# Three sets of transposes taken from TensorE to VectorE and a DRAM scratch, and 384 partial sums dealt anew, in a two-block transformer kernel

## The reference, cut to what matters

```python
q = (_rmsnorm(c_q, q_norm) @ w_qb).reshape(b, s, MLA_HEADS, MLA_QK)      # first block, layer 1
q_rope = _rope(q_rope, cos[:, :, None, :], sin[:, :, None, :])           # 16 heads x 64
mod = c_act @ w_ada[l] + b_ada[l]                                        # 2048 -> 6 x 2048, one row
qa = apply_rope(rms_norm(qa, q_norm_w[l]), cos, sin)                     # second block, 8 heads x 128
merged = jax.nn.sigmoid(ga) * (ya @ w_oa[l]) + jax.nn.sigmoid(gb) * (yb @ w_ob[l])
x = x + g1 * (merged @ w_out[l])
```

## Time and profile before

| | |
|---|---|
| median of three runs | 2192.4 us |
| the profiled execution, own time | 2195.33 us |
| its span | 2193.4 us |
| TensorE busy | 2170.4 us, 99% |
| VectorE busy | 1514.1 us, 69% |
| ScalarE busy | 1019.5 us, 46% |
| moved by DMA | 512.22 MB, mean 234 GB/s |
| granted clock of TensorE | 0.998 of 2.4 GHz |

### The profile page before, as it was taken

One profiled execution on the slowest core, in us unless ns is written; L12 is line 12 of the kernel. 1 busy time (PEld: TensorE's weight loads), 2 busy tenths in 40 slices (PEclk: granted clock), 3 DMA queues, 4 the chain that ended last, 5 costly groups with the idle time before them and its releaser, 6 DMA issues.

```text
span 2193.4 us, 32090 instructions
## 1 busy us (share of the span) xinstructions
PE 2170.4 (99%) x10814; PEld 1840.6 (84%) x10814; DVE 1514.1 (69%) x2046; ACT 1019.5 (46%) x1251; POOL 297.4 (14%) x555
## 2 busy tenths in 40 slices
PE   9999999999999999999999999999999999999998
PEld 8898888988778887899888888888888888888886
DVE  6766668877777877688776768776666666554544
ACT  5445544554444546434555544454444444444433
POOL 2101110112220010701110211111111111000000
PEclk9999999999999999999999999999999999999999
DMA  8877577688996584968766887767878887765564
GB/s 291 240 193 245 174 260 245 198 227 287 299 297 190 176 303 143 263 204 263 229 187 193 285 277 239 237 222 237 268 253 278 268 260 241 224 233 185 190 198 139
DMA packets 204124, 512.22 MB, mean 234 GB/s; under 512 B 32704, under 2 KB 60000, under 8 KB 203744
## 3 DMA queue, kind: packets, MB, share of 16 engines
q1 hardware_dynamic: 166256, 394.10, 56.3%
q0 software_dynamic: 37456, 115.92, 16.6%
q10 hardware_dynamic: 288, 0.52, 0.1%
HBM read 502.58 MB, written 7.91 MB: 233 GB/s over the span
## 4 chain that ended last, share of the span: by engine, by line
PE 89%; DMA 4%; DVE 4%; ACT 1%; issue 1%; POOLq 0%; DVEq 0%; SPq 0%; ACTq 0%
PE ps L2361 72%; PE ps L2405 10%; DMA ada_raw<-in_w_ada_dram 3%; DVE lo L1307 1%; DMA raw<-in_ml_w_in_dram 1%; DVE acc_s L1319 1%; PE ps L2458 1%; PE ps L2831 1%; PE ps L2820 1%; PE ps L2719 0%; ACT hi L736 0%; DVE acc_g L1319 0%; PE ps L2553 0%; PE ps L2501 0%; PE ps L2554 0%
## 5 line engine op out<-in xcount | busy, mean ns | idle before, releaser
L1307 DVE TENSOR_TENSOR lo<-raw,hi 128x1024 fp32r<-128x1024 f32 x731 | 890.4, 1223 | 565.8 <-ACT hi L736 563.4
L736 ACT CAST hi<-raw 128x1024 fp32r<-128x1024 f32 x731 | 765.6, 1051 | 1004.0 <-PE ps L2361 769.5
L2361 PE MATMUL ps<-hi,XH 128*128 128x512 f32 x1944 | 607.7, 392 | 6.7 <-DVE lo L1307 4.4
L2361 PE MATMUL ps<-lo,XH 128*128 128x512 f32 x1944 | 602.0, 389 | 0.0
L2361 PE MATMUL ps<-hi,XL 128*128 128x512 f32 x1944 | 601.4, 389 | 0.0
L2361 PEld LDWEIGHTS ps<-hi,XH 128*128 128x128 f32 x1944 | 361.1, 188 | 83.0 <-issue 6.4
L2361 PEld LDWEIGHTS ps<-lo,XH 128*128 128x128 f32 x1944 | 364.9, 188 | 76.7
L2361 PEld LDWEIGHTS ps<-hi,XL 128*128 128x128 f32 x1944 | 364.9, 188 | 76.7
L625 POOL DMA_DIRECT2D ada_raw<-in_w_ada_dram x304 | 163.4, 539 | 1131.8 <-DVE acc_s L1319 848.5
L1319 DVE SCALAR_TENSOR_TENSOR acc_s<-ada_raw,c_act,acc_s 128x512 f32<-128x512 f32 x256 | 191.1, 747 | 21.8 <-DMA ada_raw<-in_w_ada_dram 20.4
L2405 PE MATMUL ps<-XH,hi 128*128 (+1 forms) x504 | 142.7, 283 | 0.0
(11 more groups left out here) (394 smaller groups left out, 1910.8 us busy)
## 6 DMA issues: line engine op xcount, KB each, us to landing
ada_raw<-in_w_ada_dram POOLq DMA_DIRECT2D x384, 256.0 KB, 4.7
raw<-in_w_in_dram SPq DMA_DIRECT2D x136, 512.0 KB, 4.5
raw<-in_ml_w_in_dram SPq DMA_DIRECT2D x128, 512.0 KB, 4.6
raw<-in_w_gate_dram SPq DMA_DIRECT2D x176, 256.0 KB, 3.0
raw<-in_w_up_dram SPq DMA_DIRECT2D x176, 256.0 KB, 3.4
raw<-in_w_down_dram SPq DMA_DIRECT2D x88, 512.0 KB, 4.3
raw<-in_mla_w_in_dram SPq DMA_DIRECT2D x47, 512.0 KB, 4.7
raw<-in_mla_w_out_dram SPq DMA_DIRECT2D x32, 512.0 KB, 4.6
```

Of the source, the lines that this page charges most:

```text
L736: nc.scalar.copy(hi[:, j, :], raw[:, j, :]).then_inc(hi_ready, 1)
L1307: nc.vector.tensor_tensor(lo[:, j, :], raw[:, j, :], hi[:, j, :].bitcast(F32), ALU.subtract) \
L2361: ins = mm(ps[:, o:o + HALF], x, w[:, b % RING, c0:c0 + HALF], start=first, stop=(k == n_rows - 1 and x is xl), skip_group_check=True)
```

## The change

Three things are done. (1) The sets `qrT` and `qaT` and the first half of `merged` are turned by `turn_squares` and `regroup` instead of TensorE; ScalarE then copies or casts them into place, and VectorE forms the low part of the merged half. For the wide tiles (2048 columns) the scratch DMAs move 1 MB each way. (2) The PSUM groups after `qrT` change places, since `qrT` and `mTa` no longer take one. (3) The sums are dealt anew, and the loads on POOL's queue are ordered around the three regroupings; `gate_hi` and `gate_split` of the first gate move behind `qb`.

```diff
-REGROUPED = () + tuple(f"ffn{_p}" for _p in range(FFN_PASSES))
+REGROUPED = ("qr", "qa", "m0",) + tuple(f"ffn{_p}" for _p in range(FFN_PASSES))
...
-    ... "mv1": 20, "mo_0": 20, "mo_1": 20, "mz0": 6, "mz1": 6, "lo0": 8, "lo1": 10,
-              "qa": 8, "kb": 12, ... "oa0": 6, "ob0": 6, "oa1": 6, "ob1": 6, "wo0": 12, "wo1": 12}
+    ... "mv1": 16, "mo_0": 15, "mo_1": 15, "mz0": 10, "mz1": 10, "lo0": 8, "lo1": 10,
+              "qa": 8, "qb": 6, "kb": 12, ... "oa0": 6, "ob0": 8, "oa1": 3, "ob1": 5, "wo0": 13, "wo1": 13}
...
# POOL
-            ada_units(0, 5)
+            ada_units(0, 1)
+            ada_to(ADA_FIRST["kv"] + RING)
+            regroup("qr", qr_regrouped[:, :], qr_turned[:, :], qr_rows)
+            ada_to(32)
+            ada_units(2, 5)
...
-            ada_units(12, 20)
-            pool.wait_ge(*complete("mTa"))
+            ada_to(ADA_FIRST["vb"] + 3 + RING)
+            regroup("qa", qa_regrouped[:, :], qa_turned[:, :], qa_rows, lambda: ada_to(ADA_FIRST["vb"] + 6 + RING))
+            ada_to(16 * 14)
+            ada_units(14, 17)
+            ada_to(ADA_FIRST["oa1"] + RING)
+            regroup("m0", merged_regrouped[:, :], merged_turned[:, :], merged_rows,
+                    lambda: ada_to(ADA_FIRST["oa1"] + 2 + RING))
+            ada_to(16 * 20)
+            pool.wait_ge(*complete("mTb"))
...
# ScalarE
-            act.wait_ge(*complete("qrT"))
+            act.wait_ge(*squares_of("qr"))
             whole("kn1", kT[:, 8:16, :].rearrange(flat))
+            act.wait_ge(*rows_of("qr"))
+            nc.scalar.copy(by_quarter(qrT, 0, MLA_H // 2), quarters(qr_regrouped[:, :])).then_inc(ev("qr_ready"), 1)
...
-            gate_hi(gate1_hi, 12)
             first4(B_QB)
             each_tok("kva", lambda t: kva_tok[:, t].rearrange(flat), width=HALF)
             rest(B_QB, 16)
+            gate_hi(gate1_hi, 12)
             first4(B_KB)
...
-                if b == 13:
-                    whole("qaT", qaT[:, :, :].rearrange(flat), HD_SCALE)
+                if b == 14:
+                    act.wait_ge(*rows_of("qa"))
+                    nc.scalar.mul(by_quarter(qaT, 0, N_A), quarters(qa_regrouped[:, :]), HD_SCALE) \
+                      .then_inc(ev("qa_ready"), 1)
...
+            act.wait_ge(*rows_of("m0"))
+            nc.scalar.copy(by_quarter(XH, 0, 8), quarters(merged_regrouped[:, :])).then_inc(ev("m_hi"), 1)
+            first4(B_WO)
+            rest_blocks(B_WO, 4, 8)
...
# VectorE
-            g = turn("qrT")
-            free(nc.vector.tensor_copy(qrT[:, :, :].rearrange(flat), ps[:, g:g + 4 * HALF]))
+            dve.wait_ge(ev("q_roped"), 2)
+            turn_squares(qr_turned[:, :], qrr_tok[:, :, :, :].rearrange("p t h e -> p t (h e)"), MLA_H // 2)
...
             rest(B_KVA, 8, "kva")
-            gate_split(gate1_hi, 1)
             first4(B_QB)
...
             rest(B_QB, 16, "qb", [wait_tables] + steps[0:10])
+            gate_split(gate1_hi, 1)
             first4(B_KB)
...
-            rest(B_VB, 16, "vb", steps[22:] + [add_window(16 * i, 16 * i + 16) for i in range(4)])
+            rest(B_VB, 16, "vb", steps[22:] + [turn_queries] + [add_window(16 * i, 16 * i + 16) for i in range(4)])
...
                 if n == 1:
                     merge_columns(name, q, (s_dve, first_tok))
+                    dve.wait_ge(ev("merged"), 2)
+                    turn_squares(merged_turned[:, :], merged[0][:, :, :], 8)
...
+                if n == 2:
+                    dve.wait_ge(ev("m_hi"), 1)
+                    nc.vector.tensor_tensor(by_quarter(XL, 0, 8), quarters(merged_regrouped[:, :]),
+                                            by_quarter(XH, 0, 8).bitcast(F32), ALU.subtract).then_inc(ev("m_lo"), 1)
+            merge_columns("ob1", 1, (ev("ob1_first"), 1))
+            lo_block(B_WO + 3, 3)
+            rest_blocks(B_WO, 4, 8, 16, "wo0")
...
# TensorE
-            pe.wait_ge(ev("q_roped"), 2)
-            transposes("qrT", [(k * SEQ + tok * P, qrr_tok[:, tok, 2 * k:2 * k + 2, :].rearrange(flat))
-                               for k in range(8) for tok in range(TOK)])
...
-                if b == 9:
-                    pe.wait_ge(ev("qk_roped"), 2)
-                    transposes("qaT", [(h * SEQ + tok * P, qa_tok[:, tok, h, :]) for h in range(N_A)
-                                       for tok in range(TOK)])
...
-            pe.wait_ge(ev("merged"), 2)
-            transposes("mTa", operand_tiles(merged[0], 0))
```

More of the change, by code:

```diff
@@ L81 @@
 TURN_PLAN = (
[L83 to L93, removed]
+    "c:dve kr@0:act krt@0:act krT@0:act z1@1:act cT@0:split8 qr@1:act qn0@0:act qn1@1:act kn0@0:dve "
+    "kn1@1:act v0@0:act v1@1:act z0@0:act mo0@0:dve mo1@1:dve "
+    "ada1a@0:act x1Ta@0:split5 mlq@1:taps8 x1Tb:split4 mlk@0:taps8 mv0:act gates:dve mv1@0:act mo_0:act mo_1:act mz0:act mz1@1:act "
+    "yTa:split8 lo0:dve yTb:split8 lo1@0:dve "
+    "ada1@1:dve hTa@1:split5 qa@0:act hTb@1:split4 kva@1:act qb:act kb:act g1@1:act kaT@1:act vb@0:act "
+    "ga0@1:act ga1@1:act gb0@1:act gb1:act oa0:dve ob0:dve oa1:dve ob1:dve wo0@0:dve mTb@1:split4 wo1@1:dve "
+    "ada2@0:dve h2Ta:split5 ffn0:product1 h2Tb@1:split4 ffn1@1:product1").split() \
+    + [f"ffn{i}:product1" for i in range(2, FFN_PASSES)] + ["down0:dve", "g2:act", "down1@0:dve"]
 GROUP = {}
@@ L124 @@
 BANKS_BEFORE = {_name: 4 * _n for _n, _name in enumerate(
-    ("cT", "x1Ta", "x1Tb", "yTa", "yTb", "hTa", "hTb", "mTa", "mTb", "h2Ta", "h2Tb"))}
+    ("cT", "x1Ta", "x1Tb", "yTa", "yTb", "hTa", "hTb", "mTb", "h2Ta", "h2Tb"))}
 TURN_COUNT = {}
@@ L129 @@
         TURN_COUNT[_name] = len(TURN_COUNT) + 1
[L132 to L135, removed]
+ADA_BESIDE = {"z1": 16, "kv": 12, "z0": 16, "mo0": 16, "mo1": 14, "mlq": 0, "mlk": 4, "mv0": 16, "mv1": 16, "mo_0": 15,
+              "mo_1": 15, "mz0": 10, "mz1": 10, "lo0": 8, "lo1": 10,
+              "qa": 8, "qb": 6, "kb": 12, "vb": 16, "ga0": 12, "ga1": 12, "gb0": 12, "gb1": 16, "oa0": 6, "ob0": 8, "oa1": 3,
+              "ob1": 5, "wo0": 13, "wo1": 13}
 for _p in range(1, 9):
@@ L342, in two_block_kernel @@
                                            "lo")}
-        mla_score, mla_turned, mla_value, mla_back = (n * HALF for n in range(4))
+        mla_score, mla_turned, mla_value, mla_back = ((4 + n) * HALF for n in range(4))
         MLA_UNITS = ((0, P), (P, 2 * P))
@@ L351, in score_slot @@
         def score_slot(u):
[L352 to L354 removed]
+            return u % 2 * HALF
+        turn_slot, value_slot = 2 * HALF, 3 * HALF
         def blk_head(h):
@@ L632, in ada_units @@
                     u0 = 1
-                with pool.Fori(u0, u1) as u:
-                    with pool.Fori(0, KD // RING) as g:
-                        four(u, g, True)
+                if u0 < u1:
+                    with pool.Fori(u0, u1) as u:
+                        with pool.Fori(0, KD // RING) as g:
+                            four(u, g, True)
                 ada_sent[0] = 16 * u1
@@ L1199, in _ @@
                 rest(B_MERGE + 72 + 8 * n, 8)
[L1200 to L1211, removed]
+            act.wait_ge(*rows_of("m0"))
+            nc.scalar.copy(by_quarter(XH, 0, 8), quarters(merged_regrouped[:, :])).then_inc(ev("m_hi"), 1)
+            first4(B_WO)
+            rest_blocks(B_WO, 4, 8)
+            g = grp("mTb")
+            for k in range(4):
+                k0 = 8 + 2 * k
+                bank_turned("mTb", k)
+                nc.scalar.copy(XH[:, k0:k0 + 2, :].rearrange(flat), ps[:, g + k * HALF:g + (k + 1) * HALF]) \
+                  .then_inc(ev("m_hi"), 1)
             rest_blocks(B_WO, 8, 16)
@@ L2118, in add_window, with turn_queries @@
                 return do
-            rest(B_VB, 16, "vb", steps[22:] + [add_window(16 * i, 16 * i + 16) for i in range(4)])
+            def turn_queries():
+                turn_squares(qa_turned[:, :], qa_tok[:, :, :, :].rearrange("p t h e -> p t (h e)"), N_A)
+            rest(B_VB, 16, "vb", steps[22:] + [turn_queries] + [add_window(16 * i, 16 * i + 16) for i in range(4)])
             first4(B_MERGE)
@@ L2206, in _ @@
                             first3(n0)
-                            split_merged("mTa", 0)
                         dve.wait_ge(*(complete(name) if tok else half_of("ob1")))
@@ L2217, in _ @@
                     merge_columns(name, q, (s_dve, first_tok))
+                    dve.wait_ge(ev("merged"), 2)
+                    turn_squares(merged_turned[:, :], merged[0][:, :, :], 8)
                 if n < 3:
                     rest(n0, 8, ("ob0", "oa1", "ob1")[n])
-            for name in ("mTa", "mTb"):
-                for k in range(1 if name == "mTa" else 0, 4):
-                    split_merged(name, k)
-                if name == "mTa":
-                    lo_block(B_WO + 3, 3)
-                    merge_columns("ob1", 1, (ev("ob1_first"), 1))
-                    rest_blocks(B_WO, 4, 8, 16, "wo0")
+                if n == 2:
[5 more added lines that the diff above has]
+            rest_blocks(B_WO, 4, 8, 16, "wo0")
```

(8 more changed lines are left out.)

46 lines of the change are left out of this document (30 added, 16 removed).

## The result

The changed kernel takes 2196.89 us in the median (2194.41 to 2199.83, 22 runs), the kernel before 2193.24 (2191.36 to 2196.6, 22 runs): ratio 1.0014, 95% interval 1.0008 to 1.002. The number is inside the forecast's range, its direction is not: forecast was 1.8 us faster, measured is 3.7 us slower. The profiled execution has a span of 2196.3 us against 2193.4, and its own time is 2197.97.

The account below looks back on a forecast made before the run. TensorE, busy 99% of the span, was taken to bound the kernel. Gains of 4.85 and 4.2 us less a loss of 7.2 made 1.85 us gained: 2190.6 us in the median, range 2183.0 to 2197.0.

Parts of the forecast that it names:

- Part 1, `qr`: Taking the transposes at `qr` off TensorE gains 2.2 us; the regrouped rows' lateness costs nothing.
- `qa` and `m0`: Taking `qaT` off TensorE gains 1.75 us, `mTa` 1.1 less 0.2; the regrouping through the scratch costs nothing.
- part 3a: Fewer sums in `mv1` to `mo_1` end TensorE's idle spans there: gain 4.2 us, between 2.5 and 4.9.
- `wo0`'s half-block: TensorE idles 1.0 us at `wo0`'s second half-block, waiting for VectorE's multiply, so `mTa` gives back only 1.1 of 2.1 us.
- the cover of `oa1` block 4: VectorE's transposes behind `ob0` delay the `lo` of this block to 1327.5; between 0 and 0.6 us lost, 0.2 taken.
- Part 2: The PSUM groups swap names and each stage waits for the same neighbour: no gain or loss.
- Part 3b: Six sums beside `qb` hold up POOL's queue, so `kb` waits for unit 12: loss 7.2 us, bounds 6.0 and 8.8.
- the landing: Unit 12's first load, wanted in `kb`, lands after 5.2 us, between 4.0 and 6.8, since SyncE's queue will be quiet.
- VectorE's pace: In `kb`, blocks 5 to 8, VectorE needs 10.5 us and TensorE 8.6, so 1.8 more is lost.
- A: Rival: POOL's queue is not late or `kb` can go on, so 9.05 us is gained: 2183.4 us, chance 0.20.
- B: Rival: the idle spans in `mv1` to `mo_1` belong to the profiled execution; gain there 0.5 to 1.5, 2193.7 us, chance 0.15.
- C: Rival: POOL issues the 64 bias loads more slowly beside a busy VectorE; `kb` loses 14.0 us: 2197.4 us, chance 0.12.

Follow-up runs that it names:

- e3: The changed kernel without the scratch's write and reads for `qa` and `m0` (values not the reference's), VectorE's transposes kept: 2192.11 us, ratio 0.9993.
- e4: The kernel before with only the new deal: 16, 15, 15 sums in `mv1`, `mo_0`, `mo_1` instead of 20 each, nothing beside `qb`: 2187.44 us, ratio 0.9977.
- e2: The changed kernel with 8 of the 64 `na_bias` loads sent ahead of load 190 on POOL: 2191.39 us, ratio 0.9998.
- e1: The changed kernel with all 64 `na_bias` loads sent ahead of the loads of sums 190 and 191 on POOL: 2190.12 us, ratio 0.9987.

## Why the prediction was wrong, step by step

- **Part 1, `qr`: right.** 2.2 forecast, 2.2 measured in the pair of profiles; ScalarE's copy of the rows started at 164.57 without a wait. The write took 5.5 us and the reads 7.9 in the median, forecast 6 and 8. In one execution of ten (e3) 1.5 of it was lost to a late copy of `v1`.
- **Part 1, `qa` and `m0`: this step failed.** "At `qa` 11 blocks lie between, at `m0` 20. I cost these at nothing." I asked only whether the rows would be there in time. They were. What was late was everything else in the rings: 2 MB more within some 20 us, beside the sums (16 in `vb`) and the weights (DMA share 0.97 at 303 GB/s after, 0.81 at 263 before, from 1031 to 1056). Cost: 1.6 in `vb`, 2.1 in `ob1`; e3, without that traffic, has neither. I had used that very argument in part 3a, to credit fewer sums, and did not put it to the 2 MB that the change adds. In `vb` the late load also stood right behind the reads in POOL's queue and was asked for 7.1 us after it was sent; how the 1.6 divides between bytes and order is open. The four transposes of 128x512 took 2.48 us, forecast 2.6; `wo0`'s half-block 1.24 with its slow restart, forecast 1.0; the cover of `oa1` block 4 held.
- **Part 2: no cost seen, not tried alone.** The last stretch is equal within 0.1. The stretch to `ada1a` is 0.6 longer, all of it a wait for ScalarE (1.38 instead of 0.79). My list of idle spans had left that one out, and those of 0.75 at 749.49 and of 0.64 and 0.94 just ahead of `qa`.
- **Part 3a: right mechanism, term too small.** 6.2 instead of 4.2 (bounds 2.5 and 4.9, both too low): idle was read from the column of idle spans instead of from starts. These numbers are e4's. The changed kernel has 0.4 more, nearly all of it a shorter wait just ahead of `qa` (0.29 instead of 0.64, which e4 keeps at 0.63); which edit shortened it is open.
- **Part 3b: right mechanism; the landing was sized by the wrong cause.** 10.3 instead of 7.2 (bounds 6.0 to 8.8). By the moment at which block 5 starts, 8.4 were lost and not 5.4: the landing was 7.8 and not 5.2. I had set aside the row of the same load behind the same bias loads, 6.8, for the argument that an idle SyncE would quicken it. It did not: 7.8 here, and 7.8 again in e2 (sent 965.58, sum at 973.36). Of the 3.0 that block 5 came later than forecast, 2.6 are this landing. SyncE sent nothing more, but its load of 970.22 took 8.9 us, nearly until POOL's had landed, and the DMA share is 0.91 from 972 to 980. What the runs show in the place of my argument is the tail of the 64 small loads: the last of them landed 0.2 us ahead of the first load of unit 12, and in the kernel before the pair is alike (6.7 and 6.8 us, sent 0.5 apart). In e1, with only the bias row just ahead, that load landed in 4.6, though a load of SyncE's was under way beside it too. Whether the order in POOL's queue or the many small packets beside it made it late was not tried.

  DMA: Bandwidth & Descriptors of the Trainium skill, in its section on queues, rings and completion order, has the rule that a DMA engine goes round the rings that have work, and I had let it speak for a faster landing once SyncE's ring is empty. That condition was not met before 979.1, so these runs do not test the rule; the measurement decides against my use of it.

  Behind block 5 the forecast had 1.8 lost to VectorE's pace, and 1.9 were. That the number fits is not the clock foreseen: 1.5 of it stood in slow matmuls, which I had not thought of, and which left less to wait for at block 8. TensorE: Matmul & The Clock Gate of the Trainium skill, in the part on the HAM clock gate, says that an idle array is clocked at 1.2 GHz and returns to 2.4 once busy again; the traces agree, with 0.51 granted behind the stop of 5.79 us and 1.00 behind those of 1.60 and, in e2, 1.32.
- **The rivals.** A fell: the queue was late. B fell: e4 has the gain in the median of eleven runs, 5.4 us where B gave 0.5 to 1.5. C did not happen: the 64 bias loads took 33.34 us, 0.531 each in the median, beside a busy VectorE, as before; C's 2197.4 is close to the measured 2196.89, by another cause. The rule of SBUF — State Buffer of the Trainium skill, section on its two separate sides, on the port pair that VectorE and GpSimd share showed no effect on them.

Forecast and pair of profiles are 4.75 us apart: 3.1 are part 3b, 3.7 the two regroupings' traffic, less 2.4 in part 3a's stretch; the remaining 0.3 are the start and `ada1a`, whose wait for ScalarE is 0.5 to 1.4 us long from execution to execution.

## What to carry over

A DMA that nobody waits for is not free: add its bytes to what its stretch already moves, and ask which other load behind it has least slack. Before a sum, a load or a step is moved later on one engine, look what stands behind it in the queue of the engine that feeds it; here six sums of 0.7 us each held 64 loads of another stage, and in e1 a new order of the loads, with the same amount of work, took back 8 of the 10.3 us. For a load's landing, look at what was sent just ahead of it on its own queue. Read TensorE's stops from the starts of its matmuls, not from the idle column.

## What I had not expected of the hardware

Behind a stop of 5.79 us TensorE ran at 0.51 of its clock for 3.3 us, behind one of 5.43 (e3) for 5.7 us, and behind stops of 1.86 us and less at full clock. A 256 KB load sent right behind the four 256 KB reads of the scratch landed after 13.1 us (`qa`) and 15.1 (`m0`), and those reads took 9.8 us (`qa`) and 11.6 (`m0`) in the median, where the 1 MB write ahead of them took 5.2 and 5.1.
